# Layer norms of a four-stage decoder step: squares summed on TensorE and VectorE, weight splits and row transposes moved beside the sum, shift folded into both operand parts

## The reference, cut to what matters

```python
def layer_norm(x, g, b):
    mu = jnp.mean(xf, axis=-1, keepdims=True)
    var = jnp.mean(jnp.square(xf - mu), axis=-1, keepdims=True)
    y = (xf - mu) * lax.rsqrt(var + LN_EPS) * g + b
...
x = layer_norm(ALPHA * x + h, W['ln1_g'][i], W['ln1_b'][i])
hid = jax.nn.relu(x @ W['mlp_up'][i])
x = layer_norm(ALPHA * x + (hid * hid) @ W['mlp_down'][i], W['ln2_g'][i], W['ln2_b'][i])
x = x + jax.nn.sigmoid(x @ W['ple_gate'][i]) * (p[i] @ W['ple_proj'][i])
```

## Time and profile before

| | us |
|---|---|
| three runs: lowest, median, highest | 4804.03, 4810.1, 4812.46 |
| the profiled execution's own time | 4807.95 |
| its span (first to last instruction) | 4806.1 |
| TensorE busy with matmuls | 4162.6 (87%) |
| VectorE busy | 1655.0 (34%) |
| ScalarE busy | 1195.5 (25%) |
| GpSimd busy | 345.8 (7%) |

### The profile page before, as it was taken

The page is one execution under the profiler, slowest core; times in us unless marked ns, Lnnn a source line. Parts: engine busy times, 40 slices in busy tenths (PEclk is TensorE's granted clock), DMA queues, the critical chain, the costliest instruction groups (busy, mean ns, idle before and its releaser), DMA issues.

```text
span 4806.1 us, 84070 instructions
## 1 busy us (share of the span) xinstructions
PE 4162.6 (87%) x35567; PEld 3689.5 (77%) x35567; DVE 1655.0 (34%) x1948; ACT 1195.5 (25%) x1610; POOL 345.8 (7%) x502
## 2 busy tenths in 40 slices
PE   7879788787778999997878988998898699999967
PEld 4656657656678999996848877777777699999957
DVE  2423515325233222234243315455443422232332
ACT  2121212222223111123202223454442312121132
POOL 1120110301100000000030001111100000000000
PEclk9979979899799999998989988999998899999989
DMA  2221111201201111111102220100101011111111
GB/s 75 62 55 30 48 49 32 80 11 37 66 27 40 45 49 40 47 42 28 33 20 81 73 77 23 40 23 25 39 6 43 27 45 45 40 46 43 36 31 59
DMA packets 305299, 206.21 MB, mean 43 GB/s; under 512 B 26280, under 2 KB 290142, under 8 KB 304926
## 3 DMA queue, kind: packets, MB, share of 16 engines
q1 hardware_dynamic: 290174, 161.38, 11.5%
q0 software_dynamic: 11200, 25.97, 2.0%
q10 hardware_dynamic: 3552, 13.41, 0.7%
HBM read 173.66 MB, written 27.04 MB: 42 GB/s over the span
## 4 chain that ended last, share of the span: by engine, by line
issue 48%; PE 26%; DVE 7%; PEld 7%; ACT 4%; POOLq 3%; DVEq 1%; ACTq 1%; PEldq 1%; POOL 1%; DMA 0%; SPq 0%
PE ps L1535 24%; PEld ps L1535 7%; ACT big L611 2%; DVE big L1002 2%; POOLq L281 1%; DVE big L1092 1%; ACT L611 1%; POOLq L511 1%; PE ps L1927 1%; POOL big L283 1%; ACTq L703 1%; DVE big L1325 1%; DVE h_hi L1002 1%; POOLq L283 0%; DVE wparts L1002 0%
## 5 line engine op out<-in xcount | busy, mean ns | idle before, releaser
L1535 PE MATMUL ps<-h_hi,wparts 128*128 128x364 f32 (+1 forms) x4992 | 1009.0, 333 | 73.2 <-DVEq L1185 55.2
L1535 PEld LDWEIGHTS ps<-h_hi,wparts 128*128 128x128 f32 x4992 | 866.6, 191 | 78.0 <-DVEq L1185 59.8
L1535 PE MATMUL ps<-x_lo,wparts 128*128 128x364 f32 (+1 forms) x3360 | 699.3, 332 | 43.4 <-DVE h_hi L1002 43.3
L1535 PE MATMUL ps<-x_hi,wparts 128*128 128x364 f32 (+1 forms) x3072 | 602.7, 331 | 67.9 <-DVEq L1185 57.1
L1535 PEld LDWEIGHTS ps<-x_lo,wparts 128*128 128x128 f32 x3360 | 582.6, 190 | 49.0 <-issue 36.0
L1535 PE MATMUL ps<-big 64*64 64x64 f32 (+6 forms) x6744 | 496.2, 271 | 135.1 <-ACTq L703 44.0
L1535 PEld LDWEIGHTS ps<-x_hi,wparts 128*128 128x128 f32 x3072 | 527.7, 190 | 69.8 <-DVEq L1185 57.7
L611 ACT ACTIVATE big<-ps 128x512 f32<-128x512 f32 (+13 forms) x306 | 194.3, 660 | 1454.4 <-PE ps L1535 447.7
L1535 PEld LDWEIGHTS ps<-big 64*64 64x64 f32 (+3 forms) x6744 | 395.9, 164 | 191.5 <-issue 50.3
L1535 PE MATMUL ps<-h_lo,wparts 128*128 128x364 f32 (+1 forms) x2112 | 472.2, 333 | 0.0
L611 ACT ACTIVATE wparts<-ring 128x1024 fp32r<-128x1024 f32 x200 | 198.3, 1001 | 780.2 <-PE ps L1535 767.8
(11 more groups left out here) (215 smaller groups left out, 3674.3 us busy)
## 6 DMA issues: line engine op xcount, KB each, us to landing
ring<-in_mlp_up SPq DMA_DIRECT2D x64, 512.0 KB, 4.0
ring<-in_mlp_down SPq DMA_DIRECT2D x64, 512.0 KB, 4.0
ring<-in_w_in_even SPq DMA_DIRECT2D x28, 512.0 KB, 7.0
rkv_scratch<-big ACTq DMA_DIRECT2D x24, 544.0 KB, 2.7
big<-rkv_scratch SPq DMA_DIRECT2D x24, 544.0 KB, 4.9
big<-in_cache_k SPq DMA_DIRECT2D x128, 64.0 KB, 1.9
big<-in_cache_k POOLq DMA_DIRECT2D x128, 64.0 KB, 2.1
big<-in_cache_v SPq DMA_DIRECT2D x128, 64.0 KB, 1.8
```

Of the source, the lines that this page charges most:

```text
L1535: return pe.matmul(out, lhsT, rhs, start=start, stop=stop, skip_group_check=True)
```

## The change

- The squares are no longer added on GpSimd. TensorE sums squares 0 to 3 one by one; VectorE adds 4 to 5 and 6 to 7, and TensorE sums these two.
- The next stage's first weights (in ple the first two units) are split on ScalarE behind the squares and on VectorE behind the two additions. In out and rout they are split ahead of the high parts.
- Scale and RSTD are applied in one VectorE instruction into `xa`. ScalarE adds the shift while it makes the high part; VectorE adds it while it makes the low part; and ScalarE adds it to `xa` itself in eight instructions behind those.
- The embedding rows' first half is transposed between square 3 and the two pair sums, the second half behind them. Their splits are made before VectorE waits for RSTD.
- The ple loop is written out as eight passes, in which the next gate's weights are split first, then this pass's sigmoid (product and addition on VectorE), then the next proj's weights. The first gate job follows the low parts k by k.
- ScalarE's mlp loop is three trips and a last one, as VectorE's was.

```diff
-                for k in range(1, KT, 2):
-                    pool.wait_ge(ln_sq, 8 * n + k + 1)
-                    pool.tensor_tensor(ln[f"SQ{k}"], ln[f"SQ{k}"], ln[f"SQ{k - 1}"], ALU.add)
-                    pool.drain().then_inc(ln_sqsum, 1)
...
+            def norm(n, src, b, stage):
                 for k in range(KT):
                     act.wait_ge(ln_xc, 8 * n + k + 1)
                     f(ln[f"SQ{k}"], xs(src, k), ACT.Square).then_inc(ln_sq, 1)
+                split_w(stage, 0, 0)
+                if n % 2:
+                    split_w(stage, 0, 1, 256)
+                    act.wait_ge(pt_tr, n)
+                    f(xs(pt_hi, 0), pset(0), ACT.Copy).then_inc(xhi_ok, 1)
                 act.wait_ge(ln_var, n + 1)
                 rsqrt_mean(ln["RSTD"], pset(1), D, EPS_LN).then_inc(ln_rstd, 1)
                 for k in range(KT):
                     act.wait_ge(ln_y, 8 * n + k + 1)
-                    f(xs(dst, k), xs(src, k), ACT.Identity, scale=par[:, g + k:g + k + 1],
-                      bias=par[:, b + k:b + k + 1]).then_inc(ln_done, 1)
-                    act.drain()
-                    f(xs(x_hi if n % 2 == 0 else h_hi, k), xs(dst, k), ACT.Copy).then_inc(xhi_ok, 1)
+                    f(xs(x_hi if n % 2 == 0 else h_hi, k), xs(xa, k), ACT.Identity,
+                      bias=par[:, b + k:b + k + 1]).then_inc(xhi_ok, 1)
+                for k in range(KT):
+                    act.wait_ge(xlo_ok, split_base(f"norm{n}") + k + 1)
+                    f(xs(xa, k), xs(xa, k), ACT.Identity, bias=par[:, b + k:b + k + 1]).then_inc(ln_done, 1)
...
-            def square(stage):
-                with act.Fori(0, 2) as i:
-                    for j in range(4):
-                        split_w(stage, i, j)
-
-            def split_rhs(n, src):
-
+            def square(stage, hi, src):
+
+                split_w(stage, 0, 0)
                 for k in range(KT):
-                    f(xs((h_hi, r_hi)[n], k), xs(src, k), ACT.Copy).then_inc(xhi_ok, 1)
+                    f(xs(hi, k), xs(src, k), ACT.Copy).then_inc(xhi_ok, 1)
+                for t in range(1, KT):
+                    split_w(stage, t // 4, t % 4)
...
+                for t in range(KT):
+                    if t + 1 < KT:
+                        split_w(stage, (t + 1) // 2, (t + 1) % 2 * 2)
+                    q, used, n = job(stage, t // 2, t % 2 * 2)
+                    act.wait_ge(job_done, n + 1)
+                    act.wait_ge(ple_ct, 8 * layer + t + 1)
+                    for src, lo, n in pieces(q):
+                        last = f(like(xs(pl["GATE"], t % 2, lo, n), lo), src, ACT.Sigmoid)
+                    last.then_inc(job_free[q], 1)
+                    act.drain().then_inc(gate_ok, 1)
+                    if t + 1 < KT:
+                        split_w(stage, (t + 1) // 2, (t + 1) % 2 * 2 + 1, 256)
...
+            def norm(n, src, g, b, stage):
                 v.wait_ge(ln_mean, n + 1)
                 for k in range(KT):
                     v.scalar_tensor_tensor(out=xs(src, k), in0=pset(0), scalar=-1.0 / D, in1=xs(src, k),
                                            op0=ALU.mult, op1=ALU.add).then_inc(ln_xc, 1)
+                for k in (5, 7):
+                    v.wait_ge(ln_sq, 8 * n + k + 1)
+                    tt(ln[f"SQ{k}"], ln[f"SQ{k}"], ln[f"SQ{k - 1}"], ALU.add).then_inc(ln_sqsum, 1)
+                split_w(stage, 0, 0)
+                if n % 2:
+                    split_w(stage, 0, 1, 256)
+                    base = split_base(f"pt{n // 2}")
+                    v.wait_ge(xhi_ok, base + 1)
+                    tt(xs(pt_lo, 0), pset(0), xs(pt_hi, 0).bitcast(F32), ALU.subtract).then_inc(xlo_ok, 1)
+                    v.wait_ge(pt_tr, n + 1)
+                    v.tensor_copy(xs(pt_hi, 1), pset(0)).then_inc(xhi_ok, 1)
+                    v.drain()
+                    tt(xs(pt_lo, 1), pset(0), xs(pt_hi, 1).bitcast(F32), ALU.subtract).then_inc(xlo_ok, 1)
                 v.drain()
                 v.wait_ge(ln_rstd, n + 1)
                 hi, lo = (x_hi, x_lo) if n % 2 == 0 else (h_hi, h_lo)
 
                 def low(k):
                     v.wait_ge(xhi_ok, split_base(f"norm{n}") + k + 1)
-                    tt(xs(lo, k), xs(xa, k), xs(hi, k).bitcast(F32), ALU.subtract).then_inc(xlo_ok, 1)
+                    v.scalar_tensor_tensor(out=xs(lo, k), in0=xs(xa, k), scalar=par[:, b + k:b + k + 1],
+                                           in1=xs(hi, k).bitcast(F32), op0=ALU.add, op1=ALU.subtract).then_inc(xlo_ok, 1)
 
                 for k in range(KT):
-                    tt(xs(src, k), xs(src, k), ln["RSTD"], ALU.mult).then_inc(ln_y, 1)
-                    if k >= 3:
-                        low(k - 3)
-                for k in range(KT - 3, KT):
+                    v.scalar_tensor_tensor(out=xs(xa, k), in0=xs(src, k), scalar=par[:, g + k:g + k + 1],
+                                           in1=ln["RSTD"], op0=ALU.mult, op1=ALU.mult).then_inc(ln_y, 1)
+                    if k >= 2:
+                        low(k - 2)
+                for k in range(KT - 2, KT):
                     low(k)
...
+                for t in range(KT):
+                    if t + 1 < KT:
+                        split_w(stage, (t + 1) // 2, (t + 1) % 2 * 2)
+                    q, used, n = job(stage, t // 2, t % 2 * 2 + 1)
+                    v.wait_ge(gate_ok, 8 * layer + t + 1)
+                    v.wait_ge(job_done, n + 1)
...
+                    v.wait_ge(ln_done, 16 * layer + 16)
+                    tt(xs(lo8, t), xs(xa, t), pl["TMP"], ALU.add).then_inc(ple_ct, 1)
+                    v.drain()
+                    if t + 1 < KT:
+                        split_w(stage, (t + 1) // 2, (t + 1) % 2 * 2 + 1, 256)
...
             def norm(n):
                 pe.wait_ge(ln_acc, n + 1)
                 wide(0, ones[:, :], accum).then_inc(ln_mean, 1)
-                for p in range(KT // 2):
-                    pe.wait_ge(ln_sqsum, 4 * n + p + 1)
-                    last = wide(1, ones[:, :], ln[f"SQ{2 * p + 1}"], p == 0, p == KT // 2 - 1)
+                for k in range(4):
+                    pe.wait_ge(ln_sq, 8 * n + k + 1)
+                    wide(1, ones[:, :], ln[f"SQ{k}"], k == 0, False)
+                if n % 2:
+                    pe.wait_ge(ln_xc, 8 * n + 8)
+                    pe.wait_ge(p_land, 16 * n + 16)
+                    rows_in(0)
+                for p in range(2):
+                    pe.wait_ge(ln_sqsum, 2 * n + p + 1)
+                    last = wide(1, ones[:, :], ln[f"SQ{2 * p + 5}"], False, p == 1)
                 last.then_inc(ln_var, 1)
                 if n % 2:
-                    pe.wait_ge(ln_done, 8 * n + 8)
+                    pe.wait_ge(xlo_ok, split_base(f"pt{n // 2}") + 1)
+                    rows_in(1)
+                    pe.wait_ge(xlo_ok, split_base(f"pt{n // 2}") + 2)
...
-                with pe.Fori(0, 4) as i:
-                    for j in range(2):
-                        dense(f"ple{layer}", i, 2 * j, h_hi, h_lo)
-                        dense(f"ple{layer}", i, 2 * j + 1, pt_hi, pt_lo, kts=2)
+                for t in range(KT):
+                    dense(f"ple{layer}", t // 2, t % 2 * 2, h_hi, h_lo, ready=None if t else normed_out)
+                    dense(f"ple{layer}", t // 2, t % 2 * 2 + 1, pt_hi, pt_lo, kts=2)
```

More of the change, by code:

```diff
@@ L985, in _ @@
             act.wait_ge(rw_out, KT)
-            split_rhs(1, xa)
-            square("rout")
-            norm(2, lo8, xa, 8, 24)
+            square("rout", r_hi, xa)
+            norm(2, lo8, 24, "mlp1")
             mlp(1)
@@ L1251, in trip @@
                             v.drain()
+                            v.wait_ge(ln_done, 16 * layer + 8)
                         if t >= KT:
```

88 lines of the change are left out of this document (29 added, 59 removed).

## The result

The kernel after takes 4669.65 us (median of four runs, 4665.95 to 4674.85) against 4809.9 for the kernel before beside it: ratio 0.9711, 95% interval 0.9694 to 0.9728. Its profiled execution took 4665.95 us, with a span of 4664.4 and a mean granted clock of 0.941.

What follows compares the result with a forecast made beforehand. TensorE was taken as the bound: its matmuls and its waits for ScalarE and VectorE chains. Savings of 7.6 + 3.7 + 12.3 + 6.2 + 43.2 + 44.5 = 117.5 us from 4807.95 gave 4690.5, stated as 4691.5; range 4674 to 4712.

Steps and rivals of the forecast that it cites:

- The step that failed: Norm 2 with mlp1: forecast to save 6.2 us, with nothing counted for mlp1's trip ends.
- Out and rout: Stages out and rout: splitting the first weights ahead of the eight copies saves 7.6 and 3.7 us.
- Sum of squares: Layer norms without GpSimd's additions: 7.0 us earlier in norm 0, 0.9 in norm 2; 0.7 and 0.1 lost in odd norms.
- Even norms behind RSTD: Norms 0 and 2, from the squares' sum to job 1's evacuation: VectorE steps 1.33 us apart, 5.3 us saved.
- S: Start of a norm's first VectorE product with RSTD, forecast 3.66 us behind the squares' sum in even norms.
- Cover of the early split: Norms: job 0's weights are split while the variance is summed; without that cover it would cost 2.4 us.
- Odd norms and ple: Norms 1 and 3 with their ple loops: passes of 15 us without stalls, saving 43.2 and 44.5 us.
- rival 2: Ple loop: stalls stay, 2.3 us at 14 passes, 32 us, so 4723; chance 0.11.
- Rival 3: Norms: clock down in the last sums, 5 us per odd norm, 1.5 per even, 13 in all, 4704; chance 0.13.
- Rival 4: Norms: VectorE steps of 1.20 us as before and a clock that stays up, 4680; chance 0.08.
- Rival 5: Ple passes: clock stays at 1.2 GHz, 28 us a pass instead of 15, so 4899; chance 0.03.

Runs made afterwards that it cites:

- pad_4: Kernel before with 4 drains of TensorE ahead of norm 2; 4793.93 us, timed again 4792.25 us (6 runs), ratio 0.9969.
- ple_only: Kernel before with only the ple passes written out in the new order, norms unchanged; 4728.52 us, ratio 0.9829.
- pad_1121: Kernel before with 1121 drains of TensorE ahead of norm 2; 4866.51 us (one run).
- experiment 1: Kernel before with only the out and rout part, first weights split ahead of the eight copies; 4799.05 us against 4808.24, ratio 0.9981.
- experiment 2: Kernel after with GpSimd's four additions of squares and their drains restored; 4682.05 us, ratio 0.9740.
- experiment 5: Kernel after with the next stage's first weights split behind the norm's high and low parts, ahead of the xa updates; 4696.99 us, ratio 0.9772.

## Why the prediction was off, point by point

**The step that failed** is the one about what the change adds. The prediction costed ple's written-out passes by the order of their splits, and took mlp1 as the same before and after. Writing a loop out of 370 instructions of TensorE as eight passes moves what follows by 1084 instructions of the list (28180 - 27096; 1121 with the rest of the change), and the next loop's start with it. The kernel before had that start two instructions ahead of a block boundary and paid 3.4 to 4.3 us at three trip ends, against 0.6 to 1.3 elsewhere, and more at a lower clock behind them (0.50 to 0.66 granted in the first 4.4 to 4.6 us of a trip, 1.00 in mlp0): 12.5 us in all (pad_4). The change took it away by luck. The rows that would have told were in the trace of before: mlp1's second and third trips take 4186.58 - 3989.41 = 197.2 and 198.1 us where mlp0's take 193. I read norm 2 as a repeat of norm 0 and did not compare the two mlps.

With 12.5 added, norm 2 with mlp1 would be forecast at 18.7 (20.4 measured) and the whole at 130: 4679, inside the range. That the loop's place is the cause is shown for the kernel before (it comes and goes with drains alone); for the change itself it is shown by ple_only and by pad_1121, which puts before's loop, by the list, where after has it. By stage the two profiles differ by 141.7 us, 24.2 more than forecast, and without the 12.5 there are 11.7 left: 8.5 of scatter in the head, 2.8 taken back in the middle and tail, and 6.0 in small terms:

- **Out and rout**: 7.3 and 3.5 us, forecast 7.6 and 3.7. Right for both; alone, in experiment 1, 7.3 and 2.8.
- **Sum of squares**: 18.2 us from the mean's start, forecast 18.0. Right in size. The prediction stood between a clock that stays up and one that falls in the gap; it fell to 0.50 in the first sums and was back for the last, here and in norms 2 and 3. That norm 2 and the odd norms gain next to nothing from it was right too (experiment 2).
- **Even norms behind RSTD**: a term mis-sized. Steps 1.26 apart, not 1.33, so job 1 came at S + 28.8, not 29.7. Job 1 itself then took 13.7 us to its evacuation (1452.88 - 1439.22), where S + 29.7 to S + 44.2 gives it 14.5: the text has 14.2 for the cold job and 0.3 that it doesn't name. Norm 0 with mlp0 gave 14.4, forecast 12.3.
- **Cover of the early split**: its price without cover was put at 2.4 us a norm; experiment 5, with the split behind all parts, has 4.5 to 10.2. This didn't enter the sum.
- **Odd norms and ple**: 45.3 and 45.1, forecast 43.2 and 44.5. Right in mechanism and size: passes of 15.00 us, the updates and the sigmoid's bank ahead of gate 1, which came 30.35 + 24.65 = 55.0 us behind the mean's start.
- **Rivals**: rival 2 (stalls stay) fell, as no gap over 0.4 us is left in the passes. Rival 3 (clock down in the last sums) fell: 12 matmuls in 4.09 us, nine transposes in 1.25, at a granted clock of 1.00. What spoke for it misread a mean: 4.46 us for 18 transposes is 0.25 each, but most started 0.21 apart. Rival 4 was half right at most: steps of 1.26, and a clock that was up in the last sums and not in the first. Rival 5 (1.2 GHz in the passes) fell with the 15.00 us.

The rule of the Trainium skill that spoke for rival 3 (TensorE: Matmul & The Clock Gate, Part 4: PE-mode transpose, transposes not counting as busy for the clock), read as rival 3 reads it, would have had the two sums behind the transposes slow. They ran at full rate. Nine transposes in 1.25 us are too little work to test the rule itself.

## What to carry to other kernels

When a change lengthens or shortens TensorE's program, every loop behind it gets a new place, and its trip ends may gain or lose some 4 us each, as mlp1's did here, for reasons that the change was not made for: compare the trips of twin loops in the trace of before (here 197 against 193 us, with waits that nothing in the profile releases), and try a few idle instructions ahead of a loop that stands at its trip ends. Count an fp32 matmul as four instructions when a place is worked out. An operand split pays when it is early enough for a job to run beside the rest of its operands, which is worth more than the split's own duration. Work that nobody waits for soon, such as the updates of `xa` here, goes behind the next job's work on its engine, even when it seems hidden.

## What the runs showed that was not expected

- A loop of TensorE (2337 instructions) whose start lay two instructions ahead of a 16.4 KB block's end waited 3.4 to 4.3 us at each trip end, against 0.6 to 1.3 elsewhere; with six ahead it waited 0.7 to 1.0 at the jump and 2.2 to 2.6 a matmul later. The fetch is one block longer (12, not 11) in both. Four drains ahead of it were worth 12.5 us.
- An fp32 matmul takes four instructions of TensorE's program (two weight loads, two matmuls), an fp32r one or a transpose two: 18625 records of each kind for 10593 matmuls in the list.
- Drains of TensorE in a row cost some 0.07 us each: 1088 instead of 4 took 4867.6 - 4792.3 = 75 us.
- Transposes of 128x128 fp32 mostly started 0.11 us apart at a granted clock of 1.00 (one lasts 0.27, nine together 1.25); those of the earlier trace rows mostly 0.21 apart, at 0.50.
- GpSimd's first addition in norm 0 is followed by 6.60 us before the next, where the others have 0.18 and 0.36, behind longer idle stretches too.
- An ACTIVATE with a pointer bias on 1088 columns took 1.20 us alone and 8.84 for eight (1.09 apart). The Trainium skill (ScalarE: Activation LUTs, What ACT_TABLE_LOAD costs) gives 1.19 for one, and the trace agrees.
